# Fifty U tiles are turned during the third branch in the room of x, and the one-hot groups are woven in from tile 72

## The reference, cut to what matters

```
mod = silu(c) @ w_ada + b_ada                      # shift, scale, gate
h = rms(x) * (1 + sc1) + sh1
z = h @ w_in                                       # all branches' inputs and gates
y_a = gated linear recurrence (hgrn2) ; y_b = attention with forget gate (fox)
y_c = gated delta rule (gdn), chunks with a triangular solve
x = x + gt1 * ((sig(g_a)*y_a + sig(g_b)*y_b + sig(g_c)*y_c) @ w_out)
h2 = rms(x) * (1 + sc2) + sh2
q = h2 @ w_q ; s = q @ keys                        # 8 heads, two halves, 128 keys each
best 16 x 16 sums -> 16 experts of 128*128 per head, g = softmax(best)
ffn = sum_k g_k * gelu(u[e_k] . h2) * v[e_k]       # u, v: 16384 rows of 1024
x = x + gt2 * ffn
```

## Time and profile before

| | us |
|---|---|
| median of 3 runs | 5232.11 (5229.25 to 5234.97) |
| profiled execution | 5229.06 |
| its span | 5226.0 |
| TensorE busy | 4874.7 (93%) |
| VectorE busy | 2944.7 (56%) |
| GpSimd busy | 1862.2 (36%) |
| DMA queue of GpSimd, share of 16 engines | 44.6% |
| DMA queue of SyncE, share of 16 engines | 36.0% |

### The profile page before, as it was taken

The page is one execution under the profiler, slowest core; times in us unless marked ns, Lnnn a source line. Parts: engine busy times, 40 slices in busy tenths (PEclk is TensorE's granted clock), DMA queues, the critical chain, the costliest instruction groups (busy, mean ns, idle before and its releaser), DMA issues.

```text
span 5226.0 us, 84081 instructions
## 1 busy us (share of the span) xinstructions
PE 4874.7 (93%) x25356; PEld 3822.6 (73%) x25356; DVE 2944.7 (56%) x5545; ACT 1067.9 (20%) x2624; POOL 1862.2 (36%) x2605
## 2 busy tenths in 40 slices
PE   8999899888999998999989998988989999989998
PEld 6887776567877775777768877765778777657776
DVE  3643332424889787666536433323348897876664
ACT  1112111210111368100011121112101114680000
POOL 4432000124554445544245220001246544454442
PEclk8999999889999999999999999998899999999999
DMA  8753779576889899999877437795768999999997
GB/s 296 235 173 116 213 235 324 150 250 232 277 309 343 334 377 326 384 412 407 323 270 253 157 116 224 239 300 169 261 211 294 312 344 345 368 322 394 416 405 280
DMA packets 723472, 1489.24 MB, mean 285 GB/s; under 512 B 64593, under 2 KB 405585, under 8 KB 721569
## 3 DMA queue, kind: packets, MB, share of 16 engines
q0 software_dynamic: 249888, 858.18, 44.6%
q1 hardware_dynamic: 473216, 626.61, 36.0%
HBM read 1315.99 MB, written 302.75 MB: 310 GB/s over the span
## 4 chain that ended last, share of the span: by engine, by line
PE 62%; DMA 12%; DVE 9%; issue 7%; SPq 4%; DVEq 4%; ACT 1%; POOL 1%; POOLq 0%; ACTq 0%
PE PS L1371 19%; PE PS L707 10%; PE PS L811 7%; DMA xT<-u_rows,arena 5%; PE PS L1246 3%; PE PS L938 3%; DVE xT L1972 2%; PE PS L1314 2%; PE PS L1265 2%; PE PS L1270 2%; DMA hT<-u_rows,arena 2%; DMA u_rows<-arena 1%; DMA ring<-in_wst 1%; PE PS L850 1%; SPq L499 1%
## 5 line engine op out<-in xcount | busy, mean ns | idle before, releaser
L1314 PE MATMUL PS<-hT,ring 128*128 128x288 f32 x4096 | 1013.6, 407 | 10.5 <-DMA ring<-in_uv 10.5
L1371 PE MATMUL PS<-arena,ring 128*128 128x288 f32 x4096 | 994.3, 406 | 0.3 <-DMA ring<-in_uv 0.3
L1371 PEld LDWEIGHTS PS<-arena,ring 128*128 128x128 f32 x4096 | 777.9, 190 | 216.5 <-DMA ring<-in_uv 1.1
L1314 PEld LDWEIGHTS PS<-hT,ring 128*128 128x128 f32 x4096 | 774.3, 191 | 218.4 <-issue 9.9
L572 POOL DMA_DIRECT2D u_rows<-arena x1024 | 564.7, 553 | 143.0 <-DVE arena L1520 59.7
L811 PE MATMUL PS<-hT,ring 128*128 128x272 f32 x2304 | 601.8, 407 | 6.3 <-DMA ring<-in_wst 6.3
L686 POOL DMA_INDIRECT xT<-u_rows,arena x410 | 418.2, 1020 | 452.9 <-DVE arena L1972 376.4
L1981 DVE SCALAR_TENSOR_TENSOR PS<-xT,arena,PS 128x1024 f32<-128x1024 f32 x344 | 443.5, 1289 | 218.8 <-DMA xT<-v_rows,arena 209.5
L1972 DVE CUSTOM_DVE_ANT_0 xT<-xT,PS 128x1024 f32<-128x1024 f32 x410 | 495.0, 1215 | 99.3 <-DMA xT<-u_rows,arena 98.5
L2190 ACT ACTIVATE arena<-PS 128x272 f32<-128x272 f32 (+12 forms) x540 | 207.8, 395 | 1509.0 <-PE PS L811 511.3
L811 PEld LDWEIGHTS PS<-hT,ring 128*128 128x128 f32 x2304 | 436.9, 197 | 98.9 <-issue 17.0
(11 more groups left out here) (402 smaller groups left out, 5809.8 us busy)
## 6 DMA issues: line engine op xcount, KB each, us to landing
ring<-in_uv SPq DMA_DIRECT2D x512, 512.0 KB, 6.4
ring<-in_wst SPq DMA_DIRECT2D x312, 512.0 KB, 5.5
u_rows<-arena POOLq DMA_DIRECT2D x1024, 128.0 KB, 4.6
v_rows<-in_uv SPq DMA_DIRECT2D x256, 512.0 KB, 6.6
arena<-in_uv POOLq DMA_DIRECT2D x216, 512.0 KB, 6.1
arena<-in_ck SPq DMA_DIRECT2D x128, 256.0 KB, 5.3
arena<-in_cvv POOLq DMA_DIRECT2D x64, 256.0 KB, 4.8
gate_tiles<-arena SPq DMA_DIRECT2D x96, 136.0 KB, 4.8
```

The lines of the kernel that those rows point to most:

```text
L1314: i = mm(PS[:, 2 + s % 2, 0:TD], ring[:, s, c, :], hD[:, c, :], start=(c == 0), stop=(c == DC - 1))
L1371: i = mm(PS[:, 2 + b, 0:TD], ring[:, s, j, :], WB[:, row, :], start=(row == 0), stop=(row == NK - 1))
```

## The change

- `N_U1, N_UX, N_U2, N_U3` become 54, 50, 24, 0. The 50 new tiles are turned during the third branch. Their two input and two output buffers are the first 4096 columns of x.
- x is stored to `x_kept` after the projection stage and loaded again when the 50 tiles are stored. VectorE waits for it before the residual of the output product.
- On VectorE, `turn_in_x` puts 6 turns before the chunks of the third branch and 11 into each of the four prompt chunks. Each waits for its load and for the store of the turn two before it.
- On GpSimd, `u_tiles_in_x` stands before the small loads of the forget gates, and so do states 0 and 1 and the reload of x.
- The query stage and the top-k blocks hold no turns any more, and SyncE no longer waits for turns at the ring.
- `I_RT`, `I_OH` become 68, 72: 56 groups are woven in, 16 are left over, and `N_EARLY` becomes 104. ScalarE waits for the turns and the top-k from tile 64 on.

```diff
--- before.py
+++ after.py
...
 C_TK = C_CD + 2048
-N_U1, N_U2, N_U3 = 54, 54, 20
-U_FIRST, U_AT_OUT = 18, N_U1 + 24
+N_U1, N_UX, N_U2, N_U3 = 54, 50, 24, 0
+N_L = N_U1 + N_UX + N_U2
+U_FIRST, U_AT_OUT = 18, N_U1 + N_UX + 24
 U_OPEN = -(-N_U3 // RING) * RING + RING
-assert N_U1 % 3 == N_U2 % 3 == 0 and N_U1 + N_U2 + N_U3 == NK and C_SC + 3 * DM <= C_IN2 and C_IN2 + 3 * DM <= C_SVI
+assert N_U1 % 6 == N_U2 % 3 == 0 and N_UX % 6 == 2 and N_L + N_U3 == NK and C_SC + 3 * DM <= C_IN2 and C_IN2 + 3 * DM <= C_SVI
...
-N_EARLY = 92
+N_EARLY = 104
 N_OH = TD // 4
-I_RT, I_OH = 80, 84
+I_RT, I_OH = 68, 72
...
     TABLE = {"u": urows, "v": vrows}
-    u_tile = lambda m: m + N_U3 if m < N_U1 + N_U2 else m - N_U1 - N_U2
+    u_tile = lambda m: m + N_U3 if m < N_L else m - N_L
...
     def u_in(m):
+        if N_U1 <= m < N_U1 + N_UX:
+            return xflat[:, DM * (m % 2):DM * (m % 2 + 1)]
...
     def u_out(m):
+        if N_U1 <= m < N_U1 + N_UX:
+            return xflat[:, DM * (2 + m % 2):DM * (3 + m % 2)]
...
     vn_ld = Sig("v_rows_laid", 16 * NK)
-    ul_ld = [Sig(f"u_tile_loaded{b}", 16 * (N_U1 + N_U2) // 3) for b in range(3)]
+    ul_ld = [Sig(f"u_tile_loaded{b}", 16 * len(range(b, N_L, 3))) for b in range(3)]
...
     dot_s, dot_v, dg_s = Sig("dots_activated", 2), Sig("first_row_weights_ready", 1), Sig("row_diagonal_ready", N_LEFT)
-    xk_st, xr_ld = Sig("x_kept", 16), Sig("x_loaded_again", 16)
+    xk_st, xr_ld = Sig("x_kept", 32), Sig("x_loaded_again", 32)
...
                 if RING <= n < N_U3 + RING:
-                    sp.wait_ge(ut_v.sem, ut_v.at(l, N_U1 + N_U2 + n - RING + 1))
+                    sp.wait_ge(ut_v.sem, ut_v.at(l, N_L + n - RING + 1))
...
+        def u_tiles_in_x(l):
+            def step(m, k, load):
+                g.wait_ge(ut_v.sem, l * NK + k * 6 + (m + 1))
+                g.nop(nofuse=True)
+                if load:
+                    u_load(l, k * 6 + (u_tile(m) + 2), m + 2)
+                u_store(k * 6 + u_tile(m), m)
+            for m in (N_U1, N_U1 + 1):
+                u_load(l, u_tile(m), m)
+            with g.Fori(0, N_UX // 6) as k:
+                for b in range(6):
+                    step(N_U1 + b, k, True)
+            for m in (N_U1 + N_UX - 2, N_U1 + N_UX - 1):
+                step(m, 0, False)
...
             g.dma_start(o["cv"][l], RO[:, 2, 0:324]).then_inc(out_st.sem, 16)
+            g.wait_ge(h_r.sem, h_r.at(l, 1))
+            g.nop(nofuse=True)
+            g.dma_start(xkept, xflat).then_inc(xk_st.sem, 16)
...
+            g.wait_ge(xk_st.sem, xk_st.at(l, 16))
+            g.nop(nofuse=True)
+            u_tiles_in_x(l)
+            g.wait_ge(g_mm.sem, g_mm.at(l, 3 * 18 + 2))
+            g.nop(nofuse=True)
+            seq_states_first(l, a["gds"], GST2)
+            for m in (N_U1 + N_UX - 2, N_U1 + N_UX - 1):
+                g.wait_ge(us_st[m % 3].sem, us_st[m % 3].at(l, 64 * (m // 3 + 1)))
+                g.nop(nofuse=True)
+            g.dma_start(xflat, xkept).then_inc(xr_ld.sem, 16)
...
-            g.wait_ge(g_mm.sem, g_mm.at(l, 3 * 18 + 2))
-            g.nop(nofuse=True)
-            seq_states_first(l, a["gds"], GST2)
...
             g.nop(nofuse=True)
-            u_tiles(l, N_U1, N_U1 + N_U2)
+            u_tiles(l, N_U1 + N_UX, N_L)
...
             g.dma_start(xkept, xflat).then_inc(xk_st.sem, 16)
-            for m in range(N_U1 + N_U2, NK):
+            for m in range(N_L, NK):
...
             g.nop(nofuse=True)
-            g.wait_ge(xk_st.sem, xk_st.at(l, 16))
+            g.wait_ge(xk_st.sem, xk_st.at(l, 32))
...
-        def headnorm(l, g):
+        def headnorm(l, g, behind=lambda: None):
...
             v.drain().then_inc(hn_rc.sem, 1)
+            behind()
...
-                n = m - N_U1 - N_U2
+                n = m - N_L
...
                 v.nop(nofuse=True)
-                if m >= 3:
-                    v.wait_ge(us_st[m % 3].sem, k * 64 + us_st[m % 3].at(l, 64 * (m // 3)))
+                last = m - 2 if N_U1 + 2 <= m < N_U1 + N_UX else m - 3
+                if last >= 0:
+                    v.wait_ge(us_st[last % 3].sem, k * 64 + us_st[last % 3].at(l, 64 * (last // 3 + 1)))
...
                 NV.transpose(u_out(m).rearrange("p (e c b) -> p e c b", e=4, c=DC), src).then_inc(ut_v.sem, 1)
+            in_x = iter(range(N_U1, N_U1 + N_UX))
+            def turn_in_x(n=1):
+                for m in itertools.islice(in_x, n):
+                    turn_u(m)
...
             v.drain().then_inc(oa_r.sem, 1)
+            turn_in_x()
...
             v.drain().then_inc(rw_g.sem, 1)
-            headnorm(l, 1)
+            turn_in_x(2)
+            headnorm(l, 1, turn_in_x)
...
                 i.then_inc(bc_v.sem, 1)
+                if j == 3:
+                    turn_in_x()
             v.drain().then_inc(gq_r.sem, 1)
+            turn_in_x()
...
                 v.drain().then_inc(g_v.sem, 1)
+                turn_in_x()
...
                 v.drain().then_inc(g_v.sem, 1)
+                turn_in_x()
...
                 cp(Wn(6), bk(5)).then_inc(g_v.sem, 1)
+                turn_in_x()
...
                 v.drain().then_inc(g_v.sem, 1)
+                turn_in_x()
...
                 v.drain().then_inc(g_v.sem, 1)
+                turn_in_x()
...
                     tt(v3(W[4]), v3(W[3]), m3(lm), ALU.mult).then_inc(g_v.sem, 1)
+                    if lv == 0:
+                        turn_in_x()
...
                     cp(Wn(5), bk(5)).then_inc(g_v.sem, 1)
+                    turn_in_x()
...
                 v.drain().then_inc(gk_r.sem, 1)
+                turn_in_x(2)
+                if p == NT - 1:
+                    assert next(in_x, None) is None
...
                     if c4 < 3:
-                        turn_u(N_U1 + c4, kc)
+                        turn_u(N_U1 + N_UX + c4, kc)
...
             v.drain()
+            v.wait_ge(xr_ld.sem, xr_ld.at(l, 16))
+            v.nop(nofuse=True)
...
                     for m in range(s * 9 // 4, (s + 1) * 9 // 4):
-                        turn_u(N_U1 + 6 + m, k * 3)
+                        turn_u(N_U1 + N_UX + 6 + m, k * 3)
...
             order = {0: 0, 1: 1}
-            at, turned = 0, N_U1 + N_U2
+            at, turned = 0, N_L
...
             rows(RANK[N_SW + NBUF + 1])
-            v.wait_ge(xr_ld.sem, xr_ld.at(l, 16))
+            v.wait_ge(xr_ld.sem, xr_ld.at(l, 32))
...
-            dots(0, 68)
-            s_.wait_ge(sc_us.sem, sc_us.at(l, 9))
-            s_.wait_ge(ut_v.sem, ut_v.at(l, N_U1 + N_U2))
+            dots(0, I_RT - 4)
+            s_.wait_ge(ut_v.sem, ut_v.at(l, N_L))
             s_.nop(nofuse=True)
-            dots(68, 76)
...
                 s_.nop(nofuse=True)
-            dots(76, I_RT)
+            dots(I_RT - 4, I_RT)
```

## The result

The changed kernel took 5252.43 us (median of 11 runs, 5239.66 to 5267.26) beside 5234.6 us for the kernel before (5229.25 to 5248.34): ratio 1.0031, 95% interval 1.0020 to 1.0043. It is slower by some 18 us. The forecast of 5276 us had the sign and more than twice the size. The profiled execution has a span of 5247.0 us, 21.0 over the one of before.

A forecast was written before the change was run, and what follows sets the result against it. TensorE, busy 93% of the span, was taken to bound the kernel. 5229 - 66 (gain) + 110 (cost) = 5273, forecast as 5276 us; 5245 to 5310 had chance 0.50, the whole range being 5205 to 5325.

The forecast's parts named there:

- the gain: U pass: routes 42.7 us earlier, less 10 us in the groups; 33 us a layer, bounds 38 to 83 in both.
- P: Period of one woven one-hot group with its U tile: 5.15 us taken, bounds 5.0 and 5.4, before 5.41.
- the stages around: Merge, output stage and x copies, outside the third branch: claimed to cost nothing.
- The cost: Third branch, prompt chunks and samples' chunk together: 45 to 70 us a layer, 55 taken, 110 in both.
- The groups: U pass: weaving 56 one-hot groups, leaving 16, takes 345 us from first group to V pass, against 335 before.
- VectorE's turns: Third branch: 44 turns in the prompt chunks, each in a gap longer than its 1.24 us, cost nothing alone.
- Their waits: Prompt chunks: turns waiting for loads and stores, 0 to 17 us a layer, counted inside the DMA engines' cost.
- The DMA engines in G: Third branch's four prompt chunks: 44 load and store pairs overfill the engines; stretch of 20 to 38 us, as ring-tile waits.
- VectorE blocks: Rival, third branch: store waits add to ring waits, 85 us or more a layer, 5336 us; chance 0.14.
- share is no limit: Rival, prompt chunks: queues' packets overlap, ring keeps up, only GpSimd's late loads cost; 5216 to 5226 us; chance 0.22.
- GpSimd's queue: Samples' chunk: forget-gate loads end at 868 us, state 2 comes late, TensorE stands 27.5 us; net 25 a layer.
- owed ring tiles must be paid in S too: Samples' chunk: ring tiles owed from the prompt chunks add to its traffic, 152 us against 123, so 29 us.

The follow-up runs named there:

- the run with turns only: Changed kernel with VectorE's 50 turns in place, without these tiles' loads, stores and waits in the third branch; its prompt chunks took 239.7 and 239.8 us per layer.
- The third buffer: Changed kernel with a third output buffer for the 50 tiles, so a turn waits for the store three before; 5235.0 us, ratio 1.0007 to the kernel before.

## Why the prediction was right or wrong

**What failed, in short.** The sign and the two sides of the sum were right; the net, 44 us, was more than twice the 21 us that the span grew by. In the sum the mis-sized term is the gain: "33 us, 66 in both" measured 38.5 and 39.1 us, mostly because P was taken at 5.15 and came out at 5.02 and 5.11. The second is the term that was put at nothing, the stages around: they took 11 us less. The cost, 55 us a layer, fits to half a us, but by luck: waits for ring tiles of 20 us or more a layer were forecast and 8.7 and 11.5 us came, a wait for state 2 of 15 to 28 us and 8.2 and 9.1 came; in their place stood VectorE's waits for stores, which the prediction had laid inside the ring's, and a lower clock, for which it had no term. TensorE's busy time for the same matmuls grew by 9.6 us in G and 13.3 in S (10.3 and 10.5 in the second layer), 23 and 21 of the 55 us.

**The groups: right in kind, 6 us a layer too small.** The routes came 43.1 us earlier (44.8 in the second layer) where the prediction had 42.7, block by block as worked out from the earlier trace rows. TensorE's waits in front of the weave, for ScalarE and for the routes, were 7.3 us in the first layer and 11.4 in the second, where it had 10. The period came out at 5.02 and 5.11 us against 5.15 taken; from the first group to the V pass it was 338.0 and 341.7 us against 345. The V pass started 38.5 and 39.1 us earlier against 33. The failed term is the choice of P in the middle of its bounds; TensorE's wait for the one-hots fell to 0.12 us a group, so the value near the floor was the one to take. The twelve rows on VectorE in the V pass were free: from its start to the end of the run it is 515.8 us, where it was 515.5.

**VectorE's turns: nothing by themselves, right** (G to 0.3 us in the run with turns only).

**Their waits: wrong.** The prediction worked out the loop of two buffers, about 8 us for two turns, compared it with 11 us on average, and let 0 to 17 us of it "lie inside the next term". Its own terms, 1.24 + 3 + 4.8, add up to 9 and not to 8. At full engines the landing grew from 4.8 to 5.9 us and the loop to 11.1 us, as long as the average itself. VectorE waited 56 us (61 in the second layer), and this, not the ring, is what TensorE felt in G.

**The DMA engines in G: right in size, wrong in place.** 20 to 38 us were worked out, 30.3 and 31.3 measured, at a share of 1.05. But the waits for ring tiles that should have carried them did not come, but for 3.2 us in the second layer. The reading that fits: the loop throttled GpSimd's traffic to just what the engines could take. The nearest rival by mechanism was "VectorE blocks", with 85 us a layer; its waits came, but in place of the ring's and not on top. The third buffer, which opens that throttle, brought them, 12.8 us. The rival "share is no limit" falls: it needed a pair below 2.1 us, and a pair took 2.6 to 2.9, where the prediction had 2.6 to 3.0; at a share of 1.06 the engines moved 371 GB/s. The Trainium skill ("DMA: Bandwidth & Descriptors", section "Bandwidth"), with 436 GB/s, had made the traffic fit; the same section also puts the side of the memory at about 358 GB/s for traffic between it and SBUF, by which the 413 GB/s would not have fitted, and the prediction left that out. The rows lie between the two: 371 GB/s here and 402 in the V pass.

**GpSimd's queue: the mechanism right, the sum lucky.** The small loads ended at 895.7, not 868, as G had grown; but S1 was already 15 us longer, so TensorE stood 8.2 us for state 2 and not 27.5. S grew by 25.1 and 23.6 us where 25 to 32 were said: 15 and 7 in S1 (6 us of ring waits and the clock in the first layer), 10 and 17 in S2. The run with the gate loads between the turns takes 11 and 15 us of S2 away. The other half, "owed ring tiles must be paid in S too", was wrong as the main cause of the ring waits: with no tile traffic in G, the run with turns only still waits 7.5 us for ring tiles, and its S is 18 us over before. The reload of x makes up nearly 5 us, as moving it behind S shows.

**The sum.** G and S cost 55.4 and 54.9 us against 55. Of the 23 us by which the span grew less than forecast (44 against 21), 12 are the groups. The other 11 are in stages where TensorE's own work was not changed: from S to the U pass 561.1 us became 554.3 in the first layer, and from the V pass to the second layer's G 1039.1 became 1035.0, and the first G starts 1.0 us earlier. Of the 6.8 us of the first, 4.8 are busy time for the same matmuls, at a granted clock of 0.90 beside 0.89. In the changed kernel and the three timed runs that leave this stretch as it is there it took 548 to 554 us, in those with copies of V moved into it 545 to 563 (595 and 597 with forty in the merge), and before the change 552 us in the second layer. The 561.1 was at the high end, and the prediction, made against one profiled execution, could not know it. How much of the 11 us is chance and how much comes of the emptier query stage, which held 30 turns before, no run here separates.

## What to carry to other kernels

Work out the loop of a pair of buffers in full (the operation, the issuing of its transfers, their landing under the load that the change itself brings) and compare it with the closest spacing, not with the mean; where it comes near, it is a term of its own. Then ask what demand the loop lets through: where it just fills the DMA engines, a further buffer and less other traffic each give little alone (5 to 9 us a layer here) and together somewhat more than the sum (16 to 20). Add a term for the clock where a change brings new waits of several us to TensorE: here it was two fifths of the cost. A mean share with room in it is no room for a queue in strict order, and an engine's time saved is worth only what the next engine's order of work can do with it. And test what a stage owes to the stage before it with a run that leaves the first one's traffic out.

## What was unexpected

- A store of 4 KB landed in 3.9 us and one of 128 KB in 3.8 us at a share of 0.75 to 0.78; at 1.05 the latter took 5.9 us.
- Short waits of TensorE cost more than their length. Behind 5.46 and 3.27 us of waiting eight matmuls took 3.97 and 3.96 instead of 2.10 us. A wait of 2.5 us in the same chunk before the change left the granted clock of S1 at 1.00. In S1 the clock fell from 1.00 to 0.79 and the busy time of the same 321 matmuls rose from 31.6 to 40.3 us, more than the 6.2 us of added waits; in G it was 9.6 us on 20.7 us of waits.
- The DMA engines moved 364 to 371 GB/s in G at shares of 1.05 and 1.06, and 326 to 336 GB/s in S before the change at 1.05 to 1.07; a full stage shows a share a little over 1.
